# Residual tiles multiplied before their norm's root is known, in three stages of a two-block transformer kernel, and one weight split moved ahead behind layer norms

## The chip, the core and the metric

The kernel runs on one core of one Trainium2 chip. The metric is the device time of one execution, in microseconds (us), the median of three runs. TensorE's granted clock stands in the profile's rows as a share of full speed; its two levels are 1.2 and 2.4 GHz.

## The reference, cut to what matters

Two transformer blocks of two layers each work on `x`, 512 tokens by 1024 features, float32. In the first block each layer is a gated feed-forward, a token mixer and a second gated feed-forward, each behind a modulation and in front of a layer norm. In the second block each layer is a mixer (layer 0 "even", layer 1 "odd"), a cross attention over 256 memory rows, and a feed-forward with a squared ReLU. Before each of these `x` goes through an RMS norm with a gain per feature. The change is in this part:

```python
def rmsnorm(x, g):
    y = xf * lax.rsqrt(jnp.mean(xf * xf, axis=-1, keepdims=True) + EPS)
    return (y * g.astype(jnp.float32)).astype(x.dtype)

def odd_mixer(h, w_in, conv_w, w_pool, pool_scale, w_out):
    gb, gc, hc, zd = _split(h @ w_in, ODD_SPLITS)     # 4 parts of 512 features
    u = gc * hc
    conv = ...                                        # causal, 3 taps, by channel
    yc = gb * conv
    yd = pool_mixer(zd, w_pool, pool_scale)           # window means less zd, a 128x128 product by group
    return jnp.concatenate([yc, yd], axis=-1) @ w_out

def mlp(h, w_up, w_down):
    return jnp.square(jax.nn.relu(h @ w_up)) @ w_down

    for i in range(DEPTH):                            # second block
        x = x + mix(rmsnorm(x, g_mix[i]))             # even_mixer for i = 0, odd_mixer for i = 1
        x = x + cross_attn(rmsnorm(x, g_xattn[i]), rmsnorm(mem, g_mem[i]), ...)
        x = x + mlp(rmsnorm(x, g_mlp[i]), w_up[i], w_down[i])
```

The root belongs to a token, the gain to a feature. A product `rmsnorm(x, g) @ w` is therefore `(x * g) @ w` times the token's root, which can also be put in after the product.

## The kernel before, in words

`x` lies transposed in SBUF: tile XR[n] holds features 128n to 128n+127 on the partitions and the 512 tokens in the free dimension. So the gain is a scalar per partition, and the root a row that has to be spread over all partitions.

Products are float32 made of three products in a rounded format. Each operand is parted into a high part (ScalarE copies it into the rounded type) and a low part (VectorE or GpSimd takes the difference), and PE multiplies high by high, low by high and high by low (`mul3`). A tile of 128 output features by 512 tokens over 1024 input features is 24 products of 128x512. The high and low parts of the normed `x` are HH and HL (events "h.hi" and "h.lo").

Weights come in 1 MB chunks of 128x2048, that is two such tiles, 48 products. SP loads them into three slots (`STAGE`, chunk j in slot j mod 3), ScalarE copies the high part into one of two slots WH (step `split`), VectorE takes the low part into WL (step `low`, 128x2048). A load waits until its slot is free: until the chunk three places earlier is parted or, for a chunk of `w_ada` (vectors of the modulation, which VectorE multiplies and adds up in `ada_rows`, 8 instructions of 128x256 and a sum), until VectorE has used it. For the two chunks that follow a layer norm the slot is held until PE has summed them up (`weight_sums`).

The order of the work is written by a planner in Python (`Plan`). It emits a list of steps; each engine runs through this list and issues its own part of each step, in that order, with semaphore waits. Nothing is reordered at run time. `take` opens a chunk and puts the `split` and `low` of the next one in front of it. `ahead` parts a chunk earlier than that; `tick` lets units in the background (attention, convolution, pooling) put in their next step. PSUM has six banks in rotation (`banks`) and two that are held; a bank is free again after its reader's event.

Behind a layer norm (`late`) the first two chunks are multiplied with raw tiles while mean and variance are worked out. Their results are copied out (`late_copy`, ScalarE) and corrected (`late`, VectorE, two instructions a tile). With `one` and `two` as chunks 1 and 2, chunk 3 is parted inside `late`; chunk 4 is parted by the `take` of chunk 3, which comes behind the corrections and, in a feed-forward, behind `act_late` and `glu_late`.

Behind an RMS norm (`rms_norm`): squares of the tiles (`xsq`), 24 products of one column for the sums (`rms_a` on PE, s_cc<-s_tmp in the profile), the root by a chain of 12 small VectorE instructions (`rsqrt`, ends at L2027), the root spread over the partitions (`spread`, 8 small products), then for each tile a multiplication with gain and root (VectorE, L2209), the high part (ScalarE) and the low part (VectorE L2032 or GpSimd L2566). The first two chunks are interleaved (`pair`), with three products of no use ahead of them (`keep`). Only from there are the tiles HH and HL there. The third chunk can be parted only when the first has been used up. There are six such norms: three in front of the mixers and cross attention that stay as they are (`g_mix` of layer 0, `g_xattn` of both), and three that the change touches: `g_mlp` of layer 0, `g_mix` of layer 1 (in front of the odd mixer), `g_mlp` of layer 1.

In the odd mixer the eight chunks of w_in_o come in the order z, z, gc, gc, hc, hc, gb, gb. ScalarE evicts z, gc and gb, VectorE makes u = gc * hc. w_pool is a chunk of its own after the second. The convolution (`cv`, 4 instructions a tile) and the pooling are background units. Their result is parted into HH and HL by `o_part` when the last chunk is done; VectorE takes the low parts of every second tile in ODD_ORDER = (4, 5, 0, 6, 1, 7, 2, 3), GpSimd the others, and PE takes the tiles in that order.

Of the kernel before, what the change touches and what calls it, by code (L numbers as in the profile page):

```python
# [26 lines left out]
S = 512  # L27
# [14 lines left out]
NS = 3  # L42
# [63 lines left out]
class Plan:  # L106
    def __init__(self, stream):
# [13 lines left out]
        self.begun = None  # L121
        self.hfree = None
# [133 lines left out]
    def feat2(self, ch, kt, x, ver, eager=False, n=S, order=None):  # L256
        if self.begun and self.begun[0].j == ch.j:
            pair, self.begun = self.begun, None
            yield from self.rest_of(*pair)
            return  # L260
# [4 lines left out]
        yield from self.rest_of(*self.begin(ch, kt, n, x, ver, order), 0)  # L265
# [6 lines left out]
    def rest_of(self, ch, pid, kt, n, bs, x, ver, ks, first=4):  # L272

        for i in range(first, kt, 2):
# [4 lines left out]

    def pair(self, ch, x, ver):  # L280

        nxt = Chunk(self.taken, self.place.get(self.taken, 0))
        one, two = self.begin(ch, 8, S, x, ver), self.begin(nxt, 8, S, x, ver)
        for part in ((0, 3), (3, 4)):
            for ch, pid, kt, n, bs, x, ver, ks in (one, two):
                self.add("mm2", pid, ch, kt, n, bs, x, ver, ks, *part, 3 if part[0] == 0 and ch is one[0] else 0)
                self.tick()
        self.begun = two
        yield from self.rest_of(*one)
# [49 lines left out]
    def late(self, norm, names):  # L339
# [7 lines left out]
        def part(which, ch, pid, kt, n, bs, x, ver, ks, i0, i1):  # L347
            self.add("mm2", pid, ch, kt, n, bs, x, ver, ks, i0, i1, 0, (sid, s, uv, which))
# [63 lines left out]
        return out[:2], out[2:], ("proj", two[1] + 1)  # L412

# [89 lines left out]
    def ffn(self, kind, names, l, groups, gate, mean, norm=None, nxt=None, paired=True):  # L503
        total, after = (self.new(), []), None
        afree = [None, None]
        for gi, (g0, G) in enumerate(groups):
            self.av += 1
            av, a = self.av, gi % 2
            for mi in range(G // 2):
# [13 lines left out]
                both = first and paired  # L523
# [2593 lines left out]
```

## Time and profile before

| | |
|---|---|
| median of 3 runs | 3740.06 us (3737.62 to 3741.34) |
| the profiled execution | 3741.91 us, its span 3740.6 us |
| PE busy | 3592.7 us, 96% of the span, 16972 products |
| VectorE, ScalarE, GpSimd busy | 49%, 34%, 14% |
| mean granted TensorE clock | 0.971 |
| DMA | 373 MB, mean 100 GB/s |

A row of a timeline has the start in us, the duration, the engine, the line of the kernel, the operation, what it writes and reads, and in brackets how long the engine sat idle before it and what ended that. The names tell the stage: s_hh and s_hl are HH and HL, s_wh and s_wl the parts of a weight chunk, s_tmp, s_xm and s_xx scratch tiles, ps a PSUM bank, s_ny the root, s_cc constants. PE's products go through one line (L1356), so stages are told apart by time: the first block ends at about 2230 us, the even mixer lies from 2240 to 2600, cross attention of layer 0 to 2739, its feed-forward to 3102, the odd mixer to 3210, cross attention of layer 1 to 3374, its feed-forward to the end.

### The profile page before, as it was taken

The page shows a single profiled execution, that of the slowest core. Times are in us where ns is not written, and L with a number is a line of the kernel's source. Part 1 is how long each engine was busy: PE and PEld are TensorE (multiplying, and loading weights), DVE is VectorE, ACT ScalarE, POOL GpSimd, SP SyncE. Part 2 cuts the span into 40 slices and gives each one's busy share as a digit, 9 for nine tenths or more (in the row PEclk, how much of TensorE's full clock was granted, in tenths as well). Part 3 has the DMA queues.
Part 4 walks back from the last instruction along what each step waited for, and adds up shares of the span by engine and source line. Part 5 has one row for each costly group of instructions (what it writes and reads, how often), then busy time and mean ns, then how long its engine had stood idle before and what let it go on. Part 6 is the DMA issues. An engine that isn't in the chain of part 4 may idle for free.

```text
span 3740.6 us, 41529 instructions
## 1 busy us (share of the span) xinstructions
PE 3592.7 (96%) x16972; PEld 2912.7 (78%) x16972; DVE 1843.8 (49%) x3196; ACT 1268.0 (34%) x1722; POOL 517.8 (14%) x448
## 2 busy tenths in 40 slices
PE   8999989999999999999999989988999999999999
PEld 7888867788888888867778877646878887787887
DVE  4545753665556544634642344785543334564332
ACT  2222462342224222653432232335432233343222
POOL 1010220110012000211210020112121111202111
PEclk9999999999999999999999989979999999999999
DMA  6444322134433443210222221101212222212222
GB/s 247 161 155 152 107 85 84 46 124 161 163 138 113 158 154 128 90 46 34 77 90 102 89 75 68 57 1 46 79 69 101 101 90 82 101 69 79 102 96 73
DMA packets 52608, 373.45 MB, mean 100 GB/s; under 512 B 5825, under 2 KB 5953, under 8 KB 9538
## 3 DMA queue, kind: packets, MB, share of 16 engines
q1 hardware_dynamic: 52418, 370.79, 27.5%
q8 instruction: 134, 2.20, 0.2%
q14 instruction: 56, 0.46, 0.0%
HBM read 368.67 MB, written 2.10 MB: 99 GB/s over the span
## 4 chain that ended last, share of the span: by engine, by line
PE 43%; DVE 5%; ACT 2%; issue 1%; POOL 0%; DVEq 0%; ACTq 0%; POOLq 0%
PE ps L1356 42%; DVE s_wl L2039 1%; ACT s_wh L1714 0%; ACT s_tmp L1867 0%; DVE s_tmp L2313 0%; PE ps L1381 0%; DVE s_hl L2032 0%; DVE s_tmp L2303 0%; DVE s_tmp L2209 0%; DVE s_sm L2311 0%; ACT s_hh L1714 0%; DVE s_gc L2489 0%; DVE s_tmp L2436 0%; DVE s_sm L2416 0%; DVE s_bm L2418 0%
## 5 line engine op out<-in xcount | busy, mean ns | idle before, releaser
L1356 PE MATMUL ps<-s_hh,s_wh 128*128 128x512 f32 x2680 | 1072.4, 400 | 49.2 <-DVE s_wl L2039 21.6
L1356 PE MATMUL ps<-s_hl,s_wh 128*128 128x512 f32 x2680 | 1054.7, 394 | 0.0
L1356 PE MATMUL ps<-s_hh,s_wl 128*128 128x512 f32 x2680 | 1054.0, 393 | 0.0
L2039 DVE TENSOR_TENSOR s_wl<-s_stage,s_wh 128x2048 fp32r<-128x2048 f32 (+2 forms) x288 | 630.4, 2190 | 638.6 <-ACT s_wh L1714 638.4
L1714 ACT ACTIVATE s_wh<-s_stage 128x2048 fp32r<-128x2048 f32 (+1 forms) x277 | 519.6, 1876 | 636.3 <-PE ps L1356 507.4
L1356 PEld LDWEIGHTS ps<-s_hh,s_wh 128*128 128x128 f32 x2680 | 509.4, 190 | 186.4 <-issue 48.8
L1356 PEld LDWEIGHTS ps<-s_hh,s_wl 128*128 128x128 f32 x2680 | 508.9, 190 | 110.6 <-issue 0.2
L1356 PEld LDWEIGHTS ps<-s_hl,s_wh 128*128 128x128 f32 x2680 | 509.7, 190 | 105.9 <-issue 2.3
L1356 PE MATMUL ps<-s_ah,s_wh 128*128 128x512 f32 x1376 | 547.2, 398 | 0.0
L1356 PE MATMUL ps<-s_ah,s_wl 128*128 128x512 f32 x1376 | 537.4, 391 | 0.0
L1356 PE MATMUL ps<-s_al,s_wh 128*128 128x512 f32 x1376 | 536.9, 390 | 0.0
L2615 POOL TENSOR_TENSOR s_al<-s_tmp,s_ah 128x512 fp32r<-128x512 f32 x152 | 197.1, 1298 | 1691.3 <-ACT s_ah L1714 1691.3
L1356 PEld LDWEIGHTS ps<-s_ah,s_wl 128*128 128x128 f32 x1376 | 259.1, 188 | 55.3
L1356 PEld LDWEIGHTS ps<-s_al,s_wh 128*128 128x128 f32 x1376 | 259.5, 189 | 52.2 <-issue 1.2
L1356 PEld LDWEIGHTS ps<-s_ah,s_wh 128*128 128x128 f32 x1376 | 259.4, 189 | 52.0 <-issue 1.2
L1738 ACT ACTIVATE s_tmp<-ps 128x512 f32<-128x512 f32 x146 | 87.1, 597 | 443.1 <-PE ps L1356 443.0
L1714 ACT ACTIVATE s_ah<-s_tmp 128x512 fp32r<-128x512 f32 x152 | 96.1, 632 | 410.5 <-DVE s_tmp L2234 346.8
L2092 DVE TENSOR_TENSOR s_xr<-ps,s_xr 128x512 f32<-128x512 f32 x96 | 66.2, 690 | 232.9 <-PE ps L1356 232.9
L2090 DVE SCALAR_TENSOR_TENSOR s_xr<-ps,s_sm,s_xr 128x512 f32<-128x512 f32 x112 | 83.8, 749 | 171.5 <-PE ps L1356 171.2
L2055 DVE SCALAR_TENSOR_TENSOR s_tmp<-s_stage,s_cond,s_tmp 128x256 f32<-128x256 f32 x378 | 155.3, 478 | 0.0
L2234 DVE TENSOR_TENSOR s_tmp<-s_tmp,ps 128x512 f32<-128x512 f32 x82 | 56.1, 685 | 151.1 <-PE ps L1356 151.1
L2220 DVE TENSOR_TENSOR s_tmp<-s_tmp 128x512 f32<-128x512 f32 x64 | 47.1, 735 | 167.1 <-ACT s_tmp L1738 166.9
(428 smaller groups left out, 3632.2 us busy)
## 6 DMA issues: line engine op xcount, KB each, us to landing
s_stage<-in_w_ada SPq DMA_DIRECT2D x64, 1024.0 KB, 4.8
s_stage<-in_ffn_w_gate SPq DMA_DIRECT2D x44, 1024.0 KB, 4.8
s_stage<-in_ffn_w_up SPq DMA_DIRECT2D x44, 1024.0 KB, 4.8
s_stage<-in_ffn_down SPq DMA_DIRECT2D x32, 1024.0 KB, 4.8
s_stage<-in_w_up SPq DMA_DIRECT2D x32, 1024.0 KB, 4.7
s_stage<-in_down_m SPq DMA_DIRECT2D x32, 1024.0 KB, 4.8
s_stage<-in_w_in SPq DMA_DIRECT2D x24, 1024.0 KB, 4.8
s_stage<-in_ffn_down SPq DMA_DIRECT2D x16, 768.0 KB, 4.2
```

Source lines behind the costliest of these rows:

```text
L1356: return pe.matmul(out, lhs, rhs, start=start, stop=stop, skip_group_check=True)
L1714: return act.activation(out, src, ACT.Copy)
L1738: act.activation(m.tmp(q), m.bank(b), ACT.Silu if kind == "swiglu" else ACT.Relu).then_inc(*e.up("act_ffn", "act", pid))
L2039: ins = dve.tensor_tensor(m.WL[:, ws, a:z], m.STAGE[:, j % NS, a:z], m.WH[:, ws, a:z].bitcast(F32), ALU.subtract)
L2055: ins = dve.scalar_tensor_tensor(dst, w[:, k, :], cond, dst, ALU.mult, ALU.add)
L2090: ins = dve.scalar_tensor_tensor(x, m.bank(b), m.small(gate[0])[:, n:n + 1], x, ALU.mult, ALU.add)
L2092: ins = dve.tensor_tensor(x, m.bank(b), x, ALU.add)
L2220: dve.tensor_tensor(m.tmp(q), m.tmp(q), m.tmp(q), ALU.mult).then_inc(*e.up("dve_ffn", "act.sq", pid))
L2234: dve.tensor_tensor(m.tmp(q), m.tmp(q), m.bank(b), ALU.mult).then_inc(*e.up("dve_ffn", "glu", pid))
L2615: pool.tensor_tensor(m.AL[a][:, k, :], m.tmp(q), m.AH[a][:, k, :].bitcast(F32), ALU.subtract).then_inc(*e.up("pool_a", "a.lo", av, k))
```

## The change

`rms_norm` is no longer called in three places. Instead, while the projection in front of it is still running, each finished residual tile is multiplied by its gain alone and parted (`scaled_raw`, step `hg`: ScalarE high, VectorE low). The root is worked out while the first chunk is multiplied (`root`): sums after its first 24 products, the spread after its 48th. ScalarE then puts the root into RB and its square into R2 (two tiles of constants that are no longer needed). At the evictions `relu2` multiplies the bank by RB and then forms max(x, 0) * x, both on VectorE (before: ReLU on ScalarE, square on VectorE); in the odd mixer `o_copy` multiplies z and gb by RB, gc by R2 and hc by gc, all 16 on VectorE. `pair` and its `keep` are gone. The output of the cross attention is parted into OH and OL (the memory's tiles) since HH and HL are now written meanwhile. w_pool is taken after the third chunk and parted straight from its load. `ahead` looks past chunks that are not parted, and `late` calls it a third time: chunk 4 is parted in front of the copies and corrections of chunk 2.

```diff
     def ahead(self):
-        i = self.taken + 1
-        if self.stream and self.taken < self.nsplit <= i < len(self.stream) and not self.stream[i][2]:
-            self.nsplit = i + 1
-            return self.split(i)
+        for i in range(self.taken + 1, min(len(self.stream or ()), self.taken + NS)):
+            if not self.stream[i][2]:
+                if not self.taken < self.nsplit <= i:
+                    break
+                self.nsplit = i + 1
+                return self.split(i)
         return None
...
-    def pair(self, ch, x, ver):
...
         self.release(two[0], ("proj", two[1] + 1))
+        low = self.ahead()
         copies(two, 1)
         self.add("uv_out", sid, two[0], 1, uv, su)
+        if low:
+            self.add("low", *low)
         finish(1, mean, rs)
...
+    def scaled_raw(self, name, l, n, total):
+
+        self.add("hg", name, l, n, self.xv[n], self.hfree, self.hv + 1)
+        self.total("rms", *total, [n])
+
+    def root(self, total, done):
+
+        rid = self.new()
+        yield
+        st, y = self.held.take(), self.yr.take()
+        self.add("rms_a", rid, total, st, y)
+        for q, _ in total:
+            self.tmp.free(q, ("rms.st", rid))
+        self.held.free(st, ("rs.v", rid))
+        yield
+        yield
+        b = self.banks.take()
+        self.add("root", rid, y, b, self.rbfree)
+        self.yr.free(y, ("rms.rs", rid))
+        self.banks.free(b, ("rb", rid))
+        done.append(("rb", rid))
...
                     if kind == "swiglu":
+                        self.add("act", pid, b, q)
                         qs.append((q, pid))
                     else:
+                        self.add("relu2", pid, b, q, rb[0])
+                    self.banks.free(b, ("act", pid))
...
-            for t, (b, pid) in enumerate(self.pair(ch, "h", hv) if step == 0 else self.feat2(ch, 8, "h", hv)):
+            for t, (b, pid) in enumerate(self.feat2(ch, 8, "h", hv, step == 0)):
                 n = 2 * (i % 2) + t
-                self.add("o_copy", i // 2, n, pid, b)
+                self.add("o_copy", i // 2, n, pid, b, rb[0])
...
-            if i == 7:
-                ch = self.take("w_pool", 0)
-                self.add("o_wp", ch)
-                self.release(ch, ("wp", 1))
+            if i == 2:
+                ch = self.take("w_pool", 0, True)
+                self.add("o_wp", ch.j)
+                self.staged[ch.j] = [("wp", 1)]
+                self.issue(ch.j + NS)
                 self.bg.append(pool())
...
-        self.hv += 1
         for n in range(4):
-            self.add("x_part", l, n, self.hv, self.hfree)
+            self.add("x_part", l, n, list(mfree))
...
-        return self.project_out("wo_x", l * 2, 4, 512, "h", self.hv, None, "rms")
+        return self.project_out("wo_x", l * 2, 4, 512, "o", l, None, "rms", raw=("g_mlp", l))
...
         for l in range(2):
-            self.rms_norm("g_mix", l, total)
             if l == 0:
+                self.rms_norm("g_mix", l, total)
                 self.even_mixer()
             else:
-                self.odd_mixer()
+                self.odd_mixer(total)
             total = self.cross(l, ("w_out_e", "w_out_o")[l])
-            self.rms_norm("g_mlp", l, total)
-            total = self.ffn("relu2", mlp, l, MLP_GROUPS, None, "rms" if l == 0 else None)
+            total = self.ffn("relu2", mlp, l, MLP_GROUPS, None, "rms" if l == 0 else None, root=total, raw=("g_mix", 1) if l == 0 else None)
...
+    def hg(name, l, n, v, free, hv):
+        e.wait_ge(xe(n, v), free)
+        act.activation(m.HH[:, n, :], m.XR[:, n, :], ACT.Identity, scale=m.vec(name, l * 8 + n)).then_inc(
+            *e.up("act_h", "h.hi", hv, n))
+
+    def root(rid, y, b, free):
+        e.wait_ge(("rms.rs", rid), free)
+        act.activation(m.R2, m.bank(b), ACT.Square).then_inc(*e.up("act_root", "rb2", rid))
+        copy(m.RB, m.bank(b)).then_inc(*e.up("act_root", "rb", rid))
...
+    def hg(name, l, n, v, free, hv):
+        e.wait_ge(("h.hi", hv, n))
+        dve.scalar_tensor_tensor(m.HL[:, n, :], m.XR[:, n, :], m.vec(name, l * 8 + n), m.HH[:, n, :].bitcast(F32),
+                                 ALU.mult, ALU.subtract).then_inc(*e.up("dve_h", "h.lo", hv, n))
+
+    def relu2(pid, b, q, rb):
+        x = m.tmp(q)
+        e.wait_ge(("proj", pid), q.after, rb)
+        dve.tensor_tensor(x, m.bank(b), m.RB, ALU.mult).then_inc(*e.up("dve_act", "act", pid))
+        e.wait_ge(("act", pid))
+        dve.scalar_tensor_tensor(x, x, 0.0, x, ALU.max, ALU.mult).then_inc(*e.up("dve_ffn", "act.sq", pid))
...
+    def o_copy(part, n, pid, b, rb):
+        e.wait_ge(("proj", pid), rb, ("zero", 3), ("o.p", 1, n) if part == 2 else None)
+        dst, by = ((m.t["gb"][:, n, :], m.RB), (m.t["gc"][:, n, :], m.R2), (m.t["u"][:, n, 2:S + 2], m.t["gc"][:, n, :]),
+                   (m.t["z"][:, n, 16:S + 16], m.RB))[part]
+        dve.tensor_tensor(dst, m.bank(b), by, ALU.mult).then_inc(*e.up("dve_o", "o.p", part, n))
```

How this moves instructions, at three places. First VectorE behind the layer norm in front of the first feed-forward of layer 1 (first block). s_wl<-s_stage,s_wh is the low part of a chunk, s_sm<-ps the end of the weight sums of chunk 2, L2143 and L2146 the corrections of its tiles, L2224 `glu_late`, the rows with s_cond `ada_rows`. Before:

```order
L2134 TENSOR_SCALAR s_sm<-ps 128x2
L2136 COPY s_sm<-ps 128x2
L2143 SCALAR_TENSOR_TENSOR s_tmp<-ps,s_sm,s_tmp 128x512
L2146 TENSOR_TENSOR s_tmp<-s_tmp,ps 128x512
L2143 SCALAR_TENSOR_TENSOR s_tmp<-ps,s_sm,s_tmp 128x512
L2146 TENSOR_TENSOR s_tmp<-s_tmp,ps 128x512
L2224 SCALAR_TENSOR_TENSOR s_tmp<-s_tmp,s_sm 128x512 x2
L2039 TENSOR_TENSOR s_wl<-s_stage,s_wh 128x2048
L2052 TENSOR_SCALAR s_tmp<-s_stage,s_cond 128x256 x2
L2055 SCALAR_TENSOR_TENSOR s_tmp<-s_stage,s_cond,s_tmp 128x256 x6
```

After:

```order
L2161 TENSOR_SCALAR s_sm<-ps 128x2
L2163 COPY s_sm<-ps 128x2
L2066 TENSOR_TENSOR s_wl<-s_stage,s_wh 128x2048
L2170 SCALAR_TENSOR_TENSOR s_tmp<-ps,s_sm,s_tmp 128x512
L2173 TENSOR_TENSOR s_tmp<-s_tmp,ps 128x512
L2170 SCALAR_TENSOR_TENSOR s_tmp<-ps,s_sm,s_tmp 128x512
L2173 TENSOR_TENSOR s_tmp<-s_tmp,ps 128x512
L2258 SCALAR_TENSOR_TENSOR s_tmp<-s_tmp,s_sm 128x512 x2
L2079 TENSOR_SCALAR s_tmp<-s_stage,s_cond 128x256 x2
L2082 SCALAR_TENSOR_TENSOR s_tmp<-s_stage,s_cond,s_tmp 128x256 x6
```

The low part of chunk 4 went from behind the corrections and `glu_late` to in front of them; `ada_rows` stays behind all of them.

Second PE at the norm in front of the last feed-forward. Before:

```order
L1356 MATMUL ps<-s_hh,s_wl 128x512
L1356 MATMUL ps<-s_cc,s_tmp 128x1 x12
L1356 MATMUL ps<-s_cc,s_ny 128x128 x4
L1356 MATMUL ps<-s_cc 128x256 x3
L1356 MATMUL ps<-s_hh,s_wh 128x512
```

After, the last product ahead of the sums, and those on both sides of the spread, which comes 24 products later:

```order
L1381 MATMUL ps<-s_hh,s_wl 128x512
L1381 MATMUL ps<-s_cc,s_tmp 128x1 x12
L1381 MATMUL ps<-s_hh,s_wh 128x512
```

```order
L1381 MATMUL ps<-s_hh,s_wl 128x512
L1381 MATMUL ps<-s_cc,s_ny 128x128 x4
L1381 MATMUL ps<-s_hh,s_wh 128x512
```

Sums and spread now stand between products, and the three products of no use are gone. (The profile counts each of these small products twice.)

Third VectorE at the end of the odd mixer. s_gb<-ps,s_c is the eviction of a gb tile by RB, s_gc the convolution of a tile (L2487, L2489, L2492 before; L2526, L2528, L2531 after), s_xo the window mean of the last pooling group, s_hl<-s_po the low parts of the output. Before:

```order
L2487 TENSOR_SCALAR s_gc<-s_u,s_vec 128x512
L2492 TENSOR_TENSOR s_gc<-s_gc,s_gb 128x512
L2489 SCALAR_TENSOR_TENSOR s_gc<-s_u,s_vec,s_gc 128x512 x2
L2492 TENSOR_TENSOR s_gc<-s_gc,s_gb 128x512
L2032 TENSOR_TENSOR s_hl<-s_po,s_hh 128x512 x3
```

After:

```order
L2552 TENSOR_TENSOR s_xo<-s_xo,s_z 128x512
L2531 TENSOR_TENSOR s_gc<-s_gc,s_gb 128x512
L2515 TENSOR_TENSOR s_gb<-ps,s_c 128x512
L2526 TENSOR_SCALAR s_gc<-s_u,s_vec 128x512
L2528 SCALAR_TENSOR_TENSOR s_gc<-s_u,s_vec,s_gc 128x512 x2
L2526 TENSOR_SCALAR s_gc<-s_u,s_vec 128x512
L2531 TENSOR_TENSOR s_gc<-s_gc,s_gb 128x512
L2528 SCALAR_TENSOR_TENSOR s_gc<-s_u,s_vec,s_gc 128x512 x2
L2531 TENSOR_TENSOR s_gc<-s_gc,s_gb 128x512
L2059 TENSOR_TENSOR s_hl<-s_po,s_hh 128x512 x3
```

All of the convolution of the last two tiles now stands behind the eviction of the last projected tile, and the last pooling group's mean has moved to just ahead of it.

## Rows read from the trace of the kernel before

**Rows 1.** The page, part 1: each engine's busy time and instructions.

```profile
PE 3592.7 (96%) x16972; PEld 2912.7 (78%) x16972; DVE 1843.8 (49%) x3196; ACT 1268.0 (34%) x1722; POOL 517.8 (14%) x448
```

**Rows 2.** Waits of PE: us in total, times, longest.

```profile
PE ps L1356 <- DVE s_wl L2039: 21.6, 8, 4.8
```

**Rows 3.** Timeline of PE at the norm before layer 0's MLP.

```profile
2739.02 2.73 PE L1356 MATMUL ps<-s_cc,s_tmp 128*128 128x1 f32 x24
2744.18 1.92 PE L1356 MATMUL ps<-s_cc,s_ny 128*128 128x128 f32 x8 [2.43 <-DVE s_ny L2027]
...
2774.12 0.50 PE L1356 MATMUL ps<-s_hh,s_wh 128*128 128x512 f32 x1 [2.68 <-DVE s_wl L2039]
```

**Rows 4.** Timeline of PE at the other two norms.

```profile
3100.01 0.39 PE L1356 MATMUL ps<-s_ah,s_wl 128*128 128x512 f32 x1
...
3102.28 1.95 PE L1356 MATMUL ps<-s_cc,s_tmp 128*128 128x1 f32 x17
...
3139.65 0.80 PE L1356 MATMUL ps<-s_hh,s_wh 128*128 128x512 f32 x1 [4.81 <-DVE s_wl L2039]
...
3374.24 1.95 PE L1356 MATMUL ps<-s_cc,s_tmp 128*128 128x1 f32 x17
...
3409.47 0.50 PE L1356 MATMUL ps<-s_hh,s_wh 128*128 128x512 f32 x1 [2.68 <-DVE s_wl L2039]
```

**Rows 5.** Windows: stretch, length, busy PE PEld DVE ACT POOL, PEclk, DMA share, GB/s.

```profile
2774.10:2781.10 7.00, 6.98 (x24) 5.57 (x25) 3.31 (x3) 3.56 (x4) 2.57 (x2) 0.76 0.44 152
...
3139.60:3146.60 7.00, 6.95 (x22) 5.64 (x23) 4.19 (x5) 1.34 (x2) 1.23 (x1) 0.70 0.80 288
3409.50:3416.50 7.00, 7.00 (x24) 5.58 (x25) 3.31 (x3) 3.56 (x4) 2.58 (x2) 0.76 0.43 150
2637.30:2644.30 7.00, 7.00 (x47) 7.00 (x47) 4.16 (x13) 0.76 (x3) 0.00 (x0) 0.76 0.40 133
3271.70:3277.50 5.80, 5.80 (x50) 5.80 (x50) 4.17 (x13) 0.69 (x3) 0.00 (x0) 1.00 0.33 119
```

**Rows 6.** Timeline of PE behind three layer norms.

```profile
791.71 0.61 PE L1356 MATMUL ps<-s_hh,s_wh 128*128 128x512 f32 x1 [3.55 <-DVE s_wl L2039]
...
1178.42 0.80 PE L1356 MATMUL ps<-s_hh,s_wh 128*128 128x512 f32 x1 [3.53 <-DVE s_wl L2039]
...
1878.47 0.79 PE L1356 MATMUL ps<-s_hh,s_wh 128*128 128x512 f32 x1 [3.64 <-DVE s_wl L2039]
```

**Rows 7.** Windows behind the same three.

```profile
791.70:798.70 7.00, 6.99 (x24) 5.57 (x25) 5.16 (x9) 3.22 (x4) 0.00 (x0) 0.76 0.69 227
1178.40:1185.40 7.00, 6.98 (x18) 5.59 (x19) 3.29 (x9) 0.01 (x1) 0.00 (x0) 0.57 0.82 295
1878.50:1885.50 7.00, 7.00 (x19) 5.53 (x20) 2.29 (x1) 3.17 (x3) 0.00 (x0) 0.59 0.66 227
```

**Rows 8.** Timeline around layer 1's first feed-forward: ACT, then PE.

```profile
1187.11 1.92 ACT L1714 ACTIVATE s_wh<-s_stage 128x2048 fp32r<-128x2048 f32 x1 [8.71 <-DMA s_stage<-in_ffn_w_gate]
...
1192.24 0.39 PE L1356 MATMUL ps<-s_hh,s_wh 128*128 128x512 f32 x1
```

**Rows 9.** Timeline of PE in the first mixer of layer 0.

```profile
473.67 1.05 PE L1356 MATMUL ps<-s_nk,s_cc 128*128 128x128 f32 x4 [4.22 <-POOL s_nk L2627]
```

**Rows 10.** Timeline at the end of the odd mixer: PE, then DVE.

```profile
3212.63 0.77 PE L1356 MATMUL ps<-s_hh,s_wh 128*128 128x512 f32 x1 [2.65 <-POOL s_hl L2566]
...
3218.13 0.79 PE L1356 MATMUL ps<-s_hh,s_wh 128*128 128x512 f32 x1 [2.60 <-DVE s_hl L2032]
...
3203.62 1.54 DVE L2489 SCALAR_TENSOR_TENSOR s_gc<-s_u,s_vec,s_gc 128x512 f32<-128x512 f32 x2
...
3211.22 3.50 DVE L2489 SCALAR_TENSOR_TENSOR s_gc<-s_u,s_vec,s_gc 128x512 f32<-128x512 f32 x2
```

**Rows 11.** The page, part 5, of DVE: count, busy, mean ns, idle before.

```profile
L2039 DVE TENSOR_TENSOR s_wl<-s_stage,s_wh 128x2048 fp32r<-128x2048 f32 (+2 forms) x288 | 630.4, 2190 | 638.6 <-ACT s_wh L1714 638.4
...
L2220 DVE TENSOR_TENSOR s_tmp<-s_tmp 128x512 f32<-128x512 f32 x64 | 47.1, 735 | 167.1 <-ACT s_tmp L1738 166.9
```

More of the change, by code:

```diff
@@ L264, in feat2 @@
             return
-        yield from self.rest_of(*self.begin(ch, kt, n, x, ver, order), 0)
+        yield from self.rest_of(*self.begin(ch, kt, n, x, ver, order))
     def begin(self, ch, kt, n, x, ver, order=None):
@@ L270, in begin, with rest_of @@
         return ch, self.pid - 1, kt, n, bs, x, ver, list(order or range(kt))
-    def rest_of(self, ch, pid, kt, n, bs, x, ver, ks, first=4):
-        for i in range(first, kt, 2):
+    def rest_of(self, ch, pid, kt, n, bs, x, ver, ks):
+        for i in range(0, kt, 2):
             self.add("mm2", pid, ch, kt, n, bs, x, ver, ks, i, i + 2)
@@ L278, in rest_of @@
         yield bs[1], pid + 1
-    def pair(self, ch, x, ver):
[L282 to L289, printed above, removed]
     def toks(self, ch, kt, nc, tiles, x, ver, c0=0, n=None):
@@ L500, in rms_norm, with ffn @@
             meanwhile[1]()
-    def ffn(self, kind, names, l, groups, gate, mean, norm=None, nxt=None, paired=True):
-        total, after = (self.new(), []), None
+    def ffn(self, kind, names, l, groups, gate, mean, norm=None, nxt=None, root=None, raw=None):
+        total, after, rb = (self.new(), []), None, []
+        if root:
+            self.active.append(self.root(root, rb))
         afree = [None, None]
@@ L558, in ffn @@
                         self.raw(after, 2 * c + t)
+                    if raw and gi == len(groups) - 1:
+                        self.scaled_raw(*raw, 2 * c + t, total)
                 self.release(ch, ("proj", pid))
                 afree[a] = ("proj", pid)
-                if gi == len(groups) - 1 and mean and not after:
+                if gi == len(groups) - 1 and mean and not after and not raw:
                     self.total(mean, *total, done[:-2] if c < 3 else done)
@@ L565, in ffn, with project_out @@
             self.small.free(gate[-1][0], ("x", NT - 1, self.xv[NT - 1]))
+        if root:
+            self.rbfree = ("act", up)
+        if raw:
+            self.hv += 1
         return after or (total if mean != "rms" else self.squares(*total))
-    def project_out(self, name, idx0, kt, nc, x, ver, gate, mean, order=None, nxt=None):
+    def project_out(self, name, idx0, kt, nc, x, ver, gate, mean, order=None, nxt=None, raw=None):
         total, done, per = (self.new(), []), [], nc // P
@@ L579, in project_out @@
                     self.raw(after, per * c + t)
+                if raw:
+                    self.scaled_raw(*raw, per * c + t, total)
             self.release(ch, ("proj", pid))
             last = c == NT // per - 1
-            if not after:
+            if not after and not raw:
                 self.total(mean, *total, done if last else done[:-2])
@@ L585, in project_out @@
         self.hfree = ("proj", pid)
+        if raw:
+            self.hv += 1
         return after or (total if mean != "rms" else self.squares(*total))
@@ L1504, in rms_a @@
         ins.then_inc(*e.up("pe_norm", "rms.st", rid))
+    def root(rid, y, b, free):
+        e.wait_ge(("rs", rid), b.after)
+        spread(m.bank(b), m.y(y), range(4)).then_inc(*e.up("pe_norm", "rms.rs", rid))
     def rms_b(rid, name, l, y, b, qs, xv, hfree, hv, low_of):
```

94 lines of the change are left out of this document (40 added, 54 removed).

## The prediction

> **What bounds the kernel now.** I read part 1 of the page first: PE is busy for 3592.7 us of the 3740.6 us span and every other engine for half of it or less [rows 1]. So the time is the number of products at their pace, plus PE's idle stretches, plus the stretches at a lower granted clock. PE's waits come next: the largest single cause is a weight chunk's low part, 21.6 us in 8 waits [rows 2]. The timeline of PE then shows where they lie. At full clock ten 128x512 products go by between 3100.01 and 3102.28, 0.227 us each [rows 4]; a chunk of 48 is 10.88 us. A stretch at lower clock costs one minus its PEclk times its length, provided that PE does not wait in it.
>
> **The three RMS norms (gain).** I take for each the stretch from the first one-column sum to the first product of the third chunk, which holds two chunks, 96 products or 21.77 us of work.
> - Before layer 0's MLP: 2739.02 to 2774.12 is 35.10 us [rows 3], so 13.33 are lost. The wait at its end is followed by 7 us at PEclk 0.76 [rows 5]: 0.24 x 7 = 1.68. Together 15.0.
> - Before the odd mixer: 3102.28 to 3139.65 is 37.37 [rows 4], 15.60 lost; then 0.30 x 7 = 2.1 at PEclk 0.70 [rows 5]. Together 17.7.
> - Before the last MLP: 3374.24 to 3409.47 is 35.23 [rows 4], 13.46 lost, and again 1.68 [rows 5]. Together 15.1.
>
> The sum is 47.8. What stays is PE's own small work: the 24 sums, 2.73 us [rows 3], and the spread, whose 1.92 us stand right behind a wait and at a lower clock [rows 3]; at full clock it is between half and all of that, and I take 1.12. So 3.85 a norm, 11.55 for three, and the gain is 47.8 - 11.55 = 36.3.
>
> Does a new wait replace the old one? The root's chain lasts about the 2.43 us that PE waited for it [rows 3], and now 24 products (5.4 us) lie over it. The tiles' parts: the last residual tile is finished one eviction after the projection's last product, then comes its high part (ScalarE) and low part (VectorE), together some 4 us at the 0.7 to 1.3 us of such instructions; the first chunk goes through both its output tiles feature by feature and asks for the eighth input tile after 42 products, 9.5 us. VectorE's added work: an up chunk costs it one low part of 2.19 and four tile instructions at 0.735 [rows 11], 5.1 of 10.88 us. These cover the edit, and each at its own cost if the cover went.
>
> The clock may not stay up. A cluster of 24 one-column products stands inside the stream already: one before 2637.3 was followed by 7 us at PEclk 0.76, one before 3271.7 by 1.00 [rows 5]. I count one chance in two of 1.68 us three times, 2.5. Taken: 33.8; bounds 31.3 (always) and 36.3 (never).
>
> The Trainium skill, "TensorE: Matmul & The Clock Gate", Part 1, says that the granted clock follows how busy the engine has been. By that rule alone sums of one column would let it fall every time and the norms would be worth 31.3; the two rows disagree with each other, so I stay between.
>
> **Behind the layer norms.** Three waits for chunk 4 are 3.55, 3.53 and 3.64 us [rows 6], with a lower clock behind them of 0.24, 0.43 and 0.41 times 7 us, that is 1.7, 3.0 and 2.9 [rows 7]. The change has chunk 4 parted ahead of the copies and corrections.
> - Second feed-forward, layer 0 (791.71): 3.55 + 1.7 = 5.2; the load two chunks on may be late by a little, 0.3. Gain 4.9, bounds 2 and 5.2.
> - Second feed-forward, layer 1 (1878.47): no `ada_rows` behind it. Gain 3.64 + 2.9 = 6.5, bounds 3 and 6.5.
> - First feed-forward, layer 1 (1178.42): here the next load waits for a slot that `ada_rows` gives back. Before, ScalarE waited 8.71 us for that load, to 1187.11, and the fifth chunk began at 1192.24 [rows 8], just in time since PE was late itself. Now the low part of chunk 4 (2.2 us) goes in front of the corrections on VectorE, behind it `glu_late` and `ada_rows` end some 1.2 us later, and so do the load and the fifth chunk's low part, which then is there at about 1192.6. Without its first wait PE wants it at 1178.42 - 3.7 + 10.88 = 1185.6. The wait moves: the end is 0.4 later than 1192.24, and a wait of up to 7 us leaves a low clock of about 2.3 us behind it (the mean of 1.7 and 3.0 in rows 7). Taken: a loss of 2.7. Bounds: +3 if the load lands as it did and the clock stays, -3.
> - First mixer, layer 0: ScalarE's copies now queue behind a high part that waits for its DMA, and `ada_rows` moves 3.3 us later (one low part and the wait before it); the next w_in load, and ScalarE's chain of the gates behind it, do so too, and PE's wait of 4.22 us at 473.67 [rows 9] ends later by as much. Taken -3.3, bounds 0 and -5. In the mixer of layer 1 there is no `ada_rows`: 0.
>
> Sum: 4.9 + 6.5 - 2.7 - 3.3 = 5.4 (bounds: -3 and +14.7).
>
> **The odd mixer's end (loss).** PE has two waits there, 2.65 and 2.60 us, and takes up its sixth input tile at 3218.13 [rows 10], 8.15 us behind the last product of the projection (3212.63 - 2.65 = 3209.98). The change puts the last group's window mean behind the last chunk, so that its 128x128 product comes at about +5 us, ScalarE's high parts from +6.4, and all of the convolution of two tiles behind the eviction of the last gb tile. VectorE has then for each tile one 0.5, two together 1.54 and one 0.7 us, while GpSimd takes low parts of the output beside it: two such instructions took 1.54 us without GpSimd and 3.50 beside it [rows 10]. I get the sixth tile at about +13, a loss of 4.9. Bounds -2 (no slowing) and -8 (all of it slowed).
>
> The Trainium skill, "GPSIMD Engine Reference", Specifications, has GpSimd share its SBUF interfaces with VectorE, with contention where VectorE reads two SBUF inputs. The 3.50 us agree with it, and it speaks against the change, whose new gain-and-subtract, second `relu2` instruction and convolution all read two; without it this term would be the -2.
>
> **The sum.** 33.8 + 5.4 - 4.9 = 34.3. The profiled execution took 3741.91 us, 1.3 more than its span and 1.9 above the median of the runs, 3740.06; taken from it: 3707.6, and for a median 3705.8. I say 3706. The likeliest case's own range is 3695 to 3718.
>
> **Rivals.**
> 1. All waits go and nothing is put in their place. The 36.3 stand in full and the three layer norms give 5.2 + 6.5 + 6.5 = 18.2, with no tail and no mixer loss: 54.5, so 3686. For it: the order has little queued behind the moved parts in two of the places. Against it: the 8.71 us that ScalarE already waits for the load [rows 8].
> 2. New waits eat more. Clock low after each sum, layer norms at their lower bound, tail at -8: 31.3 - 3 - 8 = 20, so 3720. With a further wait of about 4 us in one or two of the norms (a residual tile's low part that misses its turn) 3724 to 3728. Nothing in the rows shows such a wait; the order's long queues on VectorE allow it.
> 3. It doesn't do what it says: the raw tiles' parts come so late that the first chunk waits about 11 us at each norm, 34 over three. Then no change, 3740. It would need the eighth tile 20 us behind the projection where I have 4.
> 4. VectorE becomes the bound in the 32 up chunks of the MLPs (16 a layer). It needs 5.1 us of the 10.88; from a slowing of 2.13 times on it decides. The 3.50 against 1.54 is 2.27 times [rows 10], which would be 11.6 us a chunk, +23 in all and 3729. At 2.4 times (12.2 us) it is +43, so 3749, slower. Against it: GpSimd is busy for 517.8 us of 3740.6 [rows 1], hardly in the MLPs.
>
> **Chances.** Forecast 0.62, rival 1 0.14, rival 2 0.14, rival 3 0.05, rival 4 0.05. A measurement of this kernel can tell 0.2%, 7.5 us, from no change. Faster by more: forecast, rivals 1 and 2 and a little of 4, 0.91. Within: rival 3 and some of 4, 0.06. Slower: 0.03. The range from 3688 to 3723 leaves out the far end of rival 1, part of rival 2, and rivals 3 and 4, under 2 in 10.
>
> **What the profile would show.** Right: no wait for s_ny, s_hl or s_wl of PE over 1 us in the three norms, and from the first sum to the third chunk about 25.6 us each; no wait behind the layer norms of the two second feed-forwards; a wait of 5 to 7 us at the fifth chunk of layer 1's first feed-forward, with a load behind it; the wait for s_nk about 3 us longer; at the odd mixer's end PE stands for some 10 us in all, on s_hl behind VectorE and GpSimd. Wrong: a wait in the first chunk on a raw tile's part, a granted clock under 1.00 for more than 7 us behind the sums, waits for s_ah in the up chunks, which would be VectorE's.

## The result, and the profile after

| | before | changed |
|---|---|---|
| median | 3740.70 us (4 runs, 3737.62 to 3744.23) | 3712.56 us (4 runs, 3706.90 to 3715.51) |
| ratio | | 0.9923, 95% interval 0.9905 to 0.9940 |
| profiled execution | 3741.91 us | 3711.40 us, its span 3710.1 us |

The change gives 28 us; 34 were forecast. Two more sets with the same kernel, each on another chip beside its own runs of before, gave 0.9918 (0.9902 to 0.9933) and 0.9914 (0.9901 to 0.9928), that is 30 and 31 us.

Part 1 of the page after, the row that answers to [rows 1]:

```profile
PE 3574.5 (96%) x16954; PEld 2900.3 (78%) x16954; DVE 1882.1 (51%) x3251; ACT 1226.4 (33%) x1650; POOL 498.6 (13%) x436
```

PE bounds the kernel as before. PE's waits (us in total, times, longest), which answer to [rows 2]. s_wl is a chunk's low part; s_nk is a tile of the first mixers that GpSimd masks:

```profile
PE ps L1381 <- POOL s_hl L2607: 16.9, 10, 4.8
...
PE ps L1381 <- POOL s_nk L2668: 14.1, 5, 8.2
...
PE ps L1381 <- DVE s_wl L2066: 5.0, 1, 5.0
```

Of eight waits for a chunk's low part one is left, and it is a new one; the longest wait for s_nk has grown from 4.2 to 8.2 us. PE at the norm before layer 0's MLP and at the one before the odd mixer, the timeline that answers to [rows 3, 4]:

```profile
2737.34 0.39 PE L1381 MATMUL ps<-s_hh,s_wh 128*128 128x512 f32 x1
...
2742.78 2.73 PE L1381 MATMUL ps<-s_cc,s_tmp 128*128 128x1 f32 x24
...
2750.96 1.05 PE L1381 MATMUL ps<-s_cc,s_ny 128*128 128x128 f32 x8
...
2762.77 0.39 PE L1381 MATMUL ps<-s_hh,s_wh 128*128 128x512 f32 x1
...
3094.61 2.73 PE L1381 MATMUL ps<-s_cc,s_tmp 128*128 128x1 f32 x24
...
3102.79 1.05 PE L1381 MATMUL ps<-s_cc,s_ny 128*128 128x128 f32 x8
```

No row has a bracket, so PE waited in front of none of them: the first chunk starts right behind the projection (2737.34), sums and spread stand inside the first two chunks, and the third chunk begins 25.43 us later, where 25.6 were forecast and 35.10 stood before. The spread lasts 1.05 us where 1.12 was taken. The clock behind the sums (windows, PEclk is the third number from the end) held at the first two norms and fell at the last:

```profile
2745.50:2752.50 7.00, 7.00 (x36) 5.92 (x36) 1.97 (x12) 0.45 (x1) 0.00 (x0) 1.00 0.43 150
3097.30:3104.30 7.00, 7.00 (x36) 5.92 (x36) 1.97 (x12) 0.42 (x1) 0.00 (x0) 1.00 0.32 133
3361.90:3368.90 7.00, 7.00 (x24) 5.57 (x24) 1.96 (x12) 0.00 (x0) 0.00 (x0) 0.76 0.40 150
```

The new waits. First mixer of layer 0 and first feed-forward of layer 1 (PE, ScalarE), answering to [rows 8, 9]:

```profile
478.05 1.32 PE L1381 MATMUL ps<-s_nk,s_cc 128*128 128x128 f32 x4 [8.20 <-POOL s_nk L2668]
```

```profile
469.38 1.91 ACT L1740 ACTIVATE s_wh<-s_stage 128x2048 fp32r<-128x2048 f32 x1 [7.73 <-DMA s_stage<-in_w_in]
...
1191.53 1.91 ACT L1740 ACTIVATE s_wh<-s_stage 128x2048 fp32r<-128x2048 f32 x1 [5.70 <-DMA s_stage<-in_ffn_w_gate]
```

```profile
1195.82 0.79 PE L1381 MATMUL ps<-s_hh,s_wh 128*128 128x512 f32 x1 [4.99 <-DVE s_wl L2066]
```

In both places ScalarE waits for a load that `ada_rows` let go later: the chunk's high part comes at 469.38 (465.00 before) and at 1191.53 (1187.11 before). At the odd mixer's end PE has four waits, 9.75 us in all, where it had 2.65 and 2.60 [rows 10]:

```profile
3185.74 0.79 PE L1381 MATMUL ps<-s_ph,s_wp 128*128 128x512 f32 x1 [3.48 <-POOL s_pl L2700]
...
3190.47 0.77 PE L1381 MATMUL ps<-s_hh,s_wh 128*128 128x512 f32 x1 [3.08 <-POOL s_hl L2607]
...
3194.31 0.80 PE L1381 MATMUL ps<-s_hh,s_wh 128*128 128x512 f32 x1 [0.94 <-DVE s_hl L2059]
...
3211.09 0.61 PE L1381 MATMUL ps<-s_cc,s_tmp 128*128 128x1 f32 x4 [2.25 <-POOL s_tmp L2710]
```

The projection's last product ends at 3185.74 - 3.48 = 3182.26, and the sixth tile is taken up 12.05 us behind it (8.15 before, 13 forecast). The fourth wait, for squares of the memory rows, was in no step of the forecast.

**The ledger.** To see where time goes I set each trace against the one trace of before, product by product (each has 12298 of 128x512, in the same order but for the pooling's), and read how far it is behind (+) or ahead (-). What is gained (-) or lost (+) over a stretch, in us, in thirteen traces (the changed kernel three times, and the variants below). Stretches are named by the time in the trace of before, and what was chance in that trace stands in every entry:

| stretch of before | what changed there | without that edit | with it |
|---|---|---|---|
| 440 to 480 | fourth chunk parted early, first mixer | -0.3 to +0.3 (5 traces) | +3.4 to +5.1, mean 4.1 (8) |
| 480 to 785 | nothing | -0.1 to +4.7, mean 2.5 (5) | -0.4 to +5.1, mean 2.5 (8) |
| 785 to 800 | early part, second feed-forward | 0.0 (1) | -5.5 (all 12) |
| 1140 to 1200 | early part, layer 1's first feed-forward | 0.0, -1.2, -1.2 | -0.4 to +1.5, mean 0.9 (10) |
| 1220 to 1860 | fourth chunk parted early, layer 1's first mixer | 0.0 to +5.7, mean 2.5 (5) | -6.2 to +5.8, mean 0.7 (8) |
| 1870 to 1890 | early part, second feed-forward | 0.0 (1) | -6.6 (all 12) |
| 2440 to 2480 | nothing | +6.8 (1) | -1.0 (1), +4.1 to +4.2 (11), norms changed |
| 2725 to 2785 | norm before layer 0's MLP | +0.1 (1) | -9.8 to -11.4, mean 11.0 (11) |
| 3085 to 3150 | norm before the odd mixer | -0.3 (1) | -14.0 (all 12) |
| 3150 to 3228 | the odd mixer's end | -0.3 (1) | +3.1 to +3.4, mean 3.3 (9) |
| 3228 to 3300 | the memory's sums behind it | 0.0 (1) | +0.3 to +5.6, mean 3.1 (9) |
| 3300 to 3362 | nothing | 0.0 (1) | -2.4 to 0.0, mean -1.3 (11) |
| 3362 to 3420 | last norm | 0.0 (1) | -9.8 to -11.6, mean 10.8 (11) |

(The one "without" of the rows from 2440 on is the kernel with the early parting alone. The kernel with fourfold multiplication is left out of the two norms before an MLP, and of the stretch between, since it has a wait of its own there; the three with w_pool early are left out of the rows 3150 to 3228 and 3228 to 3300, and are below. Ahead of the place of the edit, from 1139 to 1165, every trace but that of the kernel without early parting gains 1.6: so in the row 1140 to 1200 the ten are to be set against the two -1.2, not against the 0.0. The mean from 0 to 440 is -1.7.)

### The profile page after: what moved, and what is told of

It reads as the page before. It is cut to its first block and busy times, and to the rows that moved or that the text cites. A ratio compares the mean times of both kernels' runs of the same rounds, so it can differ in the third digit from the quotient of the medians.

```text
span 3710.1 us, 41485 instructions
## 1 busy us (share of the span) xinstructions
PE 3574.5 (96%) x16954; PEld 2900.3 (78%) x16954; DVE 1882.1 (51%) x3251; ACT 1226.4 (33%) x1650; POOL 498.6 (13%) x436
## 5 line engine op out<-in xcount | busy, mean ns | idle before, releaser
L1381 PE MATMUL ps<-s_hh,s_wh 128*128 128x512 f32 (+1 forms) x2616 | 1043.2, 399 | 27.5 <-POOL s_hl L2607 13.5
L1381 PE MATMUL ps<-s_hh,s_wl 128*128 128x512 f32 (+1 forms) x2616 | 1026.3, 392 | 0.0
L1381 PE MATMUL ps<-s_hl,s_wh 128*128 128x512 f32 (+1 forms) x2616 | 1026.2, 392 | 0.0
L1381 PEld LDWEIGHTS ps<-s_hh,s_wh 128*128 128x128 f32 (+1 forms) x2616 | 495.3, 189 | 157.0 <-issue 46.0
L1381 PEld LDWEIGHTS ps<-s_hh,s_wl 128*128 128x128 f32 (+1 forms) x2616 | 494.7, 189 | 107.2
L1381 PEld LDWEIGHTS ps<-s_hl,s_wh 128*128 128x128 f32 (+1 forms) x2616 | 495.8, 190 | 103.2 <-issue 2.2
L1764 ACT ACTIVATE s_tmp<-ps 128x512 f32<-128x512 f32 x82 | 48.9, 596 | 268.5 <-PE ps L1381 268.4
L1381 PEld LDWEIGHTS ps<-s_cc,s_tmp 128*128 128x128 f32 x768 | 102.9, 205 | 19.0 <-POOL s_tmp L2647 6.7
```

The costliest lines, as they stand in the source:

```text
L1381: return pe.matmul(out, lhs, rhs, start=start, stop=stop, skip_group_check=True)
L1764: act.activation(m.tmp(q), m.bank(b), ACT.Silu).then_inc(*e.up("act_ffn", "act", pid))
```

## The experiments

Three sets, each on one chip with its own runs of before (medians 3746.20, 3742.99, 3740.22 us).

### The early parting, taken away, alone, and in part

No third early parting, in `late` (e1_no_third):

```diff
-        low = self.ahead()
+        low = None
         copies(two, 1)
```

> The changed kernel without the third early parting behind layer norms: chunk 4 is parted behind the corrections again, all else stays. My theory, from the two traces: early parting wins 5.2 us and 6.2 us in the second feed-forwards and loses 10.4 us in the first mixer of layer 0 and about 2 us in layer 1's first feed-forward, so nothing is left of it and this kernel takes about 3712 us, as the changed one. Rival: the trace of one execution misleads, much of the 10.4 is chance of the clock, and the early parting is worth the 5.4 us that I forecast: 3718 us. In the profile PE's three waits of 3.5 us for the low part are back and its first wait for s_nk is 4.2 us, not 8.2.

Measured: 3714.83 us, 0.9923 (0.9910 to 0.9937), between the two theories. The three waits for the low part are back (10.7 us in all), and the longest for s_nk is 4.1 us.

The kernel before with this parting and the new `ahead` alone (e2_third_alone):

```diff
+        low = self.ahead()
         copies(two, 1)
         self.add("uv_out", sid, two[0], 1, uv, su)
+        if low:
+            self.add("low", *low)
```

> The kernel before with the third early parting behind layer norms and nothing else of the change. Same two theories from the other side: by mine 3740 us, no change against before; by the rival 3735 us. In the profile PE's wait for s_nk in the first mixer of layer 0 is about 8.2 us, the waits at chunk 4 are gone, and a wait of about 5 us stands at the fifth chunk of layer 1's first feed-forward.

Measured: 3741.58 us, 0.9985 (0.9973 to 0.9996) over 11 runs, a gain of 5.6 us (1.5 to 10), with waits of 8.14 us for s_nk and 5.07 at the fifth chunk. The interval leaves out 0, narrowly, and holds the forecast's 5.4; the ledger makes it 5.9 (below). So my theory that the early parting is worth nothing fell. The first experiment alone would not tell: 0.9923 against 0.9914 to 0.9923 of the changed kernel. The theory had failed on its 10.4 us for the first mixer: it took over from one trace the low clock behind the wait, and the ledger's second row shows that stretch to lose 2.5 us on the mean whether the edit is there or not.

In the feed-forwards only (e3_third_in_ffn, and again as e11), and in the second feed-forwards only (e4_third_in_ffn2):

```diff
-        low = self.ahead()
+        low = self.ahead() if names[0][0] != "w_in" else None
```

```diff
-        low = self.ahead()
+        low = self.ahead() if names[0][0].startswith("ffn2") else None
```

> The changed kernel with the third early parting in the feed-forwards only, not in the first mixers. My theory: the 4.0 us of PE's longer wait for s_nk come back for certain. If the stretches at a lower clock that follow it (6 more us by 668 us) hang on that wait too, the kernel takes 3702 us; the rival, that they are chance, says 3708 us. A third possibility, that the late load of w_in has another cause than ada_rows, leaves the wait at 8.2 us and the time at 3712.

> The changed kernel with the third early parting in the two second feed-forwards alone. My theory: beyond the kernel with it in all feed-forwards this gives back what the moved wait of layer 1's first feed-forward costs, about 2 us (between 0 and 3), so 3700 us; with chance clocks 3706. Rival: the wait at the fifth chunk cost less than the wait at chunk 4 that it replaced, and this kernel is 3 us slower than the one with it in all feed-forwards. The profile has the 3.5 us wait at chunk 4 there again, and no wait at the fifth.

Measured: 3705.21 us, 0.9894 (0.9880 to 0.9907), and 3704.72 us, 0.9892 (0.9877 to 0.9908). Later, on one chip with the changed kernel:

> The kernel with the third early parting in the feed-forwards only, now on one chip with the changed kernel. The wait for s_nk gives 4.0 us and the lower clock right behind it 1.1, so 5 us under the changed kernel for certain, in both traces' terms; up to 10 if the later clock stretches of that mixer hang on the wait too.

Measured: 3706.24 us, 0.9908 (0.9894 to 0.9921), beside 3708.95 us, 0.9914 (0.9901 to 0.9928): 2.7 us apart with intervals that overlap. PE in the first mixer, of e3_third_in_ffn:

```profile
473.28 1.11 PE L1381 MATMUL ps<-s_nk,s_cc 128*128 128x128 f32 x4 [4.06 <-POOL s_nk L2668]
```

The wait is back at 4.06 us in this one place. In the ledger the edit costs 4.1 us there, in layer 1's first feed-forward 2.1 (+0.9 against -1.2 without), and no more: what came above these 6 us in the first comparison, with the changed kernel on another chip, was chance. The time alone can't separate the two partial kernels.

### The changed kernel again, and its chance

> The changed kernel once more, unaltered, so that the others of this set are compared on one chip, and so that a second trace shows which stretches at a lower clock come back. If the stretches behind PE's longer wait for s_nk in the first mixer hang on that wait, PE is again about 10 us behind the kernel before by the end of that mixer; if half of them are chance, 7 or less. Time 28 to 33 us under the kernel before.

> The changed kernel unaltered, a third time, as the one to compare this set with on its chip: 28 to 33 us under the kernel before. PE's wait of 2.25 us for the squares of the memory rows (s_tmp from GpSimd) stood in one of its two traces so far; if it hangs on when the load of the memory rows lands and not on the order, it may stand here or not, with no other change at that place.

Measured: 3713.22 and 3708.95 us. Behind the s_nk wait it was 5.5 and 2.4 us behind the kernel before at 700 us, against 10.5 in the first trace: about half of those 10.5 or more was chance. The wait for s_nk itself was 6.1 and 5.6 us long where the first trace had 8.20. The 2.25 us wait for the memory's squares stood in neither.

### The end of the odd mixer

w_pool after the second chunk again (e6_pool_early, e10_pool_early_2):

```diff
-            if i == 2:
+            if i == 7:
                 ch = self.take("w_pool", 0, True)
```

> The changed kernel with w_pool taken after the second chunk of the odd mixer's projection, as before the change, so that the last pooling group's mean comes before the last chunk and not behind it. My theory: the mean's late place gives PE's wait of 3.48 us for s_pl and delays the convolutions behind it on VectorE by 1.3 us. PE's waits between the last product of the projection and the cross attention, 9.75 us in the changed kernel (3.48, 3.08, 0.94 and 2.25), fall to about 6.5, and the time by some 3 us against the changed kernel of the same set. Rival: the place of the gb eviction, now on VectorE ahead of both convolutions, sets the end, and only the 1.3 us come back; the wait for s_pl turns into a longer one for s_hl.

Measured: 3702.70 us, 0.9888 (0.9871 to 0.9906), 10.5 us under the changed kernel of its set where 3 were expected. Hence the repetition:

> The kernel with w_pool after the second chunk again. In its first trace PE's waits at the end of the odd mixer were as long as in the changed kernel of the same set (7.53 against 7.51 us, in two waits and not three), the sixth tile came only 1.0 us sooner, and yet its median was 10.5 us lower, most of it from stretches at a lower clock ahead of the odd mixer, where the two programs are the same. If that was chance of the runs, this pair comes out 1 to 4 us apart; if something in the program makes it so, again about 10.

Measured: 3706.25 us, 0.9909 (0.9895 to 0.9922), 2.7 us under the changed kernel. Most of the 10 us was chance. PE and VectorE at the odd mixer's end, of e6_pool_early:

```profile
3183.95 0.76 PE L1381 MATMUL ps<-s_hh,s_wh 128*128 128x512 f32 x1 [2.40 <-POOL s_hl L2607]
...
3191.97 0.79 PE L1381 MATMUL ps<-s_hh,s_wh 128*128 128x512 f32 x1 [5.13 <-DVE s_hl L2059]
```

```profile
3181.59 0.69 DVE L2515 TENSOR_TENSOR s_gb<-ps,s_c 128x512 f32<-128x512 f32 x1 [1.51 <-PE ps L1381]
3182.20 0.48 DVE L2526 TENSOR_SCALAR s_gc<-s_u,s_vec 128x512 f32<-128x512 f32 x1
3182.71 3.32 DVE L2528 SCALAR_TENSOR_TENSOR s_gc<-s_u,s_vec,s_gc 128x512 f32<-128x512 f32 x2
```

The wait for s_pl is gone and the others grew to the same 7.5 us: the rival held, with 0.5 us in place of its 1.3. The gb eviction, now on VectorE, and both convolutions behind it set the end, and they run beside GpSimd's low parts (3.32 us for two instructions, 1.54 alone [rows 10]). The ledger gives 0.5 us for 3150 to 3228 (+2.8 against +3.3). But from 3228 to 3300 these three traces lose 0.0 where the others lose up to 5.6. That is the fourth wait: the four traces that have it lose 5.5 to 5.6 there, the five that don't lose 0.3 or 1.8. GpSimd's last addition and VectorE in the changed kernel's first trace, then in its second (e5_changed_again):

```profile
3208.23 2.81 POOL L2710 TENSOR_TENSOR s_tmp<-s_tmp,s_xx 128x256 f32<-128x256 f32 x1
```

```profile
3208.17 2.29 DVE L2066 TENSOR_TENSOR s_wl<-s_stage,s_wh 128x2048 fp32r<-128x2048 f32 x1 [1.32 <-ACT s_wh L1740]
```

```profile
3213.41 0.74 POOL L2710 TENSOR_TENSOR s_tmp<-s_tmp,s_xx 128x256 f32<-128x256 f32 x1
```

```profile
3213.51 2.79 DVE L2066 TENSOR_TENSOR s_wl<-s_stage,s_wh 128x2048 fp32r<-128x2048 f32 x1 [1.32 <-ACT s_wh L1740]
```

The memory rows are loaded once VectorE is through with the low parts (issued at 3197.25), 15.0 us behind the projection's last product where it was 10.0 before. ScalarE and GpSimd square and add them up, and the last addition meets the low part of a weight chunk on VectorE. In the first trace it began 0.06 us behind the low part and took 2.81 us; in the second it began 0.10 us ahead of it and took 0.74, and the low part took 2.79 instead of 2.29. Whichever began second was held up. Of the nine traces with w_pool as in the change the four with the wait all have the addition 0.06 to 0.23 us behind (2.64 to 2.81 us long), the five without it all have it 0.03 to 0.10 us ahead (0.74 us). Then PE waits 2.25 us, and its granted clock is 0.76 over the 7 us behind that, where it is 1.00 in the second trace. With w_pool early the load is issued 12.3 us behind (3193.84, e6_pool_early), the addition begins 1.5 to 1.6 us ahead of the low part, and no trace of three has the wait. So the later load puts the two together, and a tenth of a microsecond decides which of them is held up. That is read from twelve traces; no run moved this addition by itself.

The Trainium skill, "GPSIMD Engine Reference", Specifications, states that GpSimd shares its SBUF interfaces with VectorE; the rows of 2.81 and 0.74 us agree, and put a price on GpSimd's side.

### How much room VectorE has in the MLPs

The multiplication by the root four times (e7_relu_x4) and twice (e12_relu_x2), in `relu2`:

```diff
+        for i in range(3):
+            dve.tensor_tensor(x, m.bank(b), m.RB, ALU.mult).then_inc(*e.up("dve_act", "act.x", pid, i))
+            e.wait_ge(("act.x", pid, i))
         dve.tensor_tensor(x, m.bank(b), m.RB, ALU.mult).then_inc(*e.up("dve_act", "act", pid))
```

(`range(1)` in the second.)

> The changed kernel with the multiplication by the root in relu2 done four times instead of once, in both MLPs: six more VectorE instructions of 0.69 us in each of 32 up chunks, so that VectorE has 5.1 + 4.1 = 9.2 us of work in a chunk of 10.9. My theory, that VectorE's time is slack there up to the length of a chunk: no change, within 3 us. Rival: a tile's chain (bank, two multiplications, high part, low part) sets the time of each group before VectorE is full; the 2.1 us more a tile then show as waits of PE for s_ah, up to 2 us at each of the 8 groups, 5 to 16 us in all.

Measured: 3762.51 us, 1.0048 (1.0033 to 1.0064): 49 us slower than the changed kernel and slower than before. Both expectations were wrong. Its waits, and VectorE, ScalarE and PE in a group:

```profile
PE ps L1381 <- POOL s_al L2659: 27.8, 16, 2.5
```

```profile
2787.14 2.29 DVE L2066 TENSOR_TENSOR s_wl<-s_stage,s_wh 128x2048 fp32r<-128x2048 f32 x1 [2.50 <-ACT s_wh L1740]
2789.35 2.13 DVE L2253 TENSOR_TENSOR s_tmp<-ps,s_c 128x512 f32<-128x512 f32 x3
...
2798.93 2.29 DVE L2066 TENSOR_TENSOR s_wl<-s_stage,s_wh 128x2048 fp32r<-128x2048 f32 x1 [2.50 <-ACT s_wh L1740]
```

```profile
2784.67 0.63 ACT L1740 ACTIVATE s_ah<-s_tmp 128x512 fp32r<-128x512 f32 x1 [2.87 <-DVE s_tmp L2257]
2785.20 1.90 ACT L1740 ACTIVATE s_wh<-s_stage 128x2048 fp32r<-128x2048 f32 x1
```

```profile
2794.99 0.50 PE L1381 MATMUL ps<-s_ah,s_wh 128*128 128x512 f32 x1 [1.11 <-POOL s_al L2659]
...
2798.49 0.79 PE L1381 MATMUL ps<-s_ah,s_wh 128*128 128x512 f32 x1 [2.54 <-POOL s_al L2659]
```

VectorE's low parts stand 2798.93 - 2787.14 = 11.79 us apart, though it idles 2.50 of them: it waits for ScalarE's high part of the chunk, which stands in ScalarE's queue behind the high part of the last tile, which waits for VectorE's own multiplications. This loop through two queues, not VectorE's busy time, has to fit into the 10.88 us that PE takes for a chunk. It misses by 0.91 a chunk, 3.65 over the four chunks of a group, and PE waits 1.11 + 2.54 = 3.65 there; 8 groups make 29 us, and the low clock behind them (0.71 over the 7 us from 2799.30) fits the rest of the ledger's 23 us an MLP.

> The changed kernel with the multiplication by the root in relu2 done twice. With it done four times VectorE was not full, yet a chunk took 11.79 us, the sum of a loop: VectorE's 10 tile instructions, ScalarE's high part of the tile (0.63) and of the next chunk (1.90) behind it, VectorE's low part of that chunk (2.29), and the next tiles only then. By this theory each repetition adds 1.42 us to the loop and 0.71 to the last tile of a group; twice means 8.95 us of loop, under the 10.88 of a chunk, and the last tile, 1.1 us early in the changed kernel, is still 0.4 early: no change, within 2 us. Rival: every multiplication added on the way to a group's last tile shows in full, 8 groups of 0.7 to 1.4 us and the lower clock behind a wait, 6 to 15 us.

Measured: 3712.97 us, 0.9927 (0.9913 to 0.9940), against 3708.95 of its set, where the intervals overlap. The ledger decides: over 2780 to 3090 and over 3416 to the end it loses 0.0 us, and PE has no wait for s_ah or s_al. By this working the loop is 11.79 - 2 x 1.42 = 8.95 us and fits.

### Both repairs

> The changed kernel with both repairs: the third early parting in the second feed-forwards alone, and w_pool after the second chunk. If the two add up: 7 to 10 us from the first, 3 from the second, so 10 to 13 us under the changed kernel of this set, and about 3700 us. Rival: the second is worth 1 us, 8 to 11 us under it.

Measured: 3700.50 us (5 runs, 3697.10 to 3702.54), 0.9880 (0.9862 to 0.9898), 12.7 us under the changed kernel of its set (0.9902 to 0.9933). It is the fastest version here and beats both kernels. By the ledger the repairs are worth 4.1 + 2.1 + 0.5 and the 3.1 behind the tail, 9.8 together; the three more are within the chance that the pairs above showed.

## Why the prediction was right, and where it was off

**The norms.** Right in every part: the first chunk waited for nothing, root and tiles' parts were covered, and of the 47.8 us 11 stayed (2.73 and 1.05 a norm). The clock was mis-sized: low behind the sums in 9 of 36 places (12 traces of changed kernels, three norms), not in half: 3 in 12, 0 in 12 and 6 in 12. Each time cost 1.6 us, where 1.68 was taken. So the norms are worth 11.0 + 14.0 + 10.8 = 35.8 us by the ledger, inside the bounds of 31.3 and 36.3, where 33.8 were forecast. Of the 2.0 more the clock is about 1.3.

**Behind the layer norms.** Forecast 4.9, 6.5, -2.7, -3.3; measured 5.5, 6.6, -2.1, -4.1. The sum is 5.9 for 5.4. The moved wait at the fifth chunk (4.99 us; 5 to 7 forecast) and the s_nk wait stand where they were put. The working for the fifth chunk took 3.7 us for a wait that rows 6 give as 3.53, which shifts its 1185.6 by 0.2 and changes nothing. The working for the mixer had the order right, ScalarE's copies behind a high part that waits for its DMA: `ada_rows` began at 460.69 (457.05 before), 3.6 us later for 3.3.

**The odd mixer's end.** Forecast 4.9 lost; measured 3.9 by the forecast's own measure (12.05 against 8.15 us) and 3.3 by the ledger, since the last pooling group's three products, which stood ahead of the last chunk before, now lie in those 12.05 us and are no loss. The contention is as expected. The step that was missing is what the tail pushes: the load of the memory rows 5 us later, and behind it a wait in some runs, 3.1 us on the mean. The forecast stopped at the sixth tile and put this term at nothing.

**The sum.** Measured terms: 35.8 + 5.9 - 3.3 - 3.1 = 35.3 us, against medians of 28, 30 and 31. The 4 to 7 us between lie in stretches where no edit shows: lost are 2.5 on the mean from 480 to 785, 1.4 from 1220 to 1860 (mean of all 12 changed kernels, -6.2 to +5.8), and 4.1 from 2440 to 2480, where all 12 traces with an early parting lose at least that; gained are 1.7 up to 440, 1.2 around 1150 and 1.3 from 3300 to 3362. That leaves 31.5, and the three traces of the changed kernel are 31.4 us ahead on the mean. That 34.3 came so near the result is partly luck: the norms gave more than forecast, the memory's wait and these stretches took more than that back. From 2440 to 2480 it is the granted clock, in windows over the same 136 products of the even mixer, before and after:

```profile
2435.00:2480.00 45.00, 39.71 (x136) 20.59 (x136) 41.68 (x126) 12.96 (x36) 6.35 (x5) 0.77 0.00 1
```

```profile
2429.00:2478.00 49.00, 42.79 (x136) 21.69 (x136) 41.82 (x126) 12.90 (x36) 6.34 (x5) 0.72 0.00 1
```

Whether the trace of before was lucky there or the shift in time brings another pattern of the clock is open: the kernel with the early parting alone shows it too, the one without any early parting does not.

**The rivals.** Rival 1 (no new waits) is out: both new waits and the tail stood. Rival 3 and the far end of rival 2 wanted a wait for a raw tile's part in the first chunk, and there is none; the rest of rival 2 wanted the clock low behind every sum and 8 us lost at the tail, and neither came. Rival 4 put its point of decision in the wrong place. It compared VectorE's busy time, 5.1 us, with 10.88; what has to fit is the loop through ScalarE's queue, 11.79 - 3 x 1.42 = 7.53 us in the changed kernel, so by this working added work shows from 3.35 us on, not from 5.8; the runs have 1.42 us added in the loop without cost and 4.26 with. With the work that I called covered, 9.2 us, the kernel was slower than before. "These cover the edit" was right for the change and its reason was too generous. GpSimd did not slow VectorE there: the multiplications took 0.69 us each.

## What to carry to other kernels

To see whether an engine has room, follow the loop through every in-order queue that its work passes, with what it waits for there, and compare that with the period: the busy share leaves out the waits inside the loop. When a stage ends later, look one stage on for what is issued at its end (a load here), since slack there is used up too. And a single pair of traces shows which waits changed, but not what they cost: the s_nk wait was 8.2, 6.1 and 5.6 us in three traces of one kernel, a wait of 2.25 us came and went by a tenth of a microsecond, and five traces without the edit and eight with it were needed to see that 2.5 us of its bill were not its own.

## What the runs showed that I had not expected

Sums of one column inside a full stream of products mostly leave the granted clock at its higher level: 27 of 36 times at 1.00, and otherwise 0.76 over 7 us. It differed by place with the same sums (0 of 12 before the odd mixer, 6 of 12 at the last norm); why is open.

Medians of four to six executions of one kernel against another in one set still misled: 10.5 us between two kernels that were 2.7 us apart when both were run again, although in the first set no run of the one reached the times of the other.
